# Prompt attention of a hybrid decoder step: stacked score products, turned probabilities as the moving operand, and segments taken from the projection's output

## What is computed

```python
s = einsum('btgrd,bngd->bgrtn', q, kc[:, :, 0]) * HEAD_DIM ** -0.5   # compressed: 31 tokens
p = masked_softmax(s, blk_last[None, :] <= qpos[:, None])
o_cmp = einsum('bgrtn,bngd->btgrd', p, kc[:, :, 1])
# selected and window: the same with 512 keys, and a causal mask
attn = gates[..., 0, None] * o_cmp + gates[..., 1, None] * o_sel + gates[..., 2, None] * o_win
```

## Time and profile before

| | us |
|---|---|
| three timed runs | 3175.24, 3179.0, 3216.62 |
| their median | 3179.0 |
| profiled execution, span (the only time the page gives for it) | 3309.7 |
| TensorE busy | 3073.8 (93%) |
| VectorE busy | 1112.6 (34%) |
| ScalarE busy | 779.8 (24%) |
| GpSimd busy | 144.8 (4%) |

### The profile page before, as it was taken

One profiled execution on the slowest core, in us unless ns is written; L12 is line 12 of the kernel. 1 busy time (PEld: TensorE's weight loads), 2 busy tenths in 40 slices (PEclk: granted clock), 3 DMA queues, 4 the chain that ended last, 5 costly groups with the idle time before them and its releaser, 6 DMA issues.

```text
span 3309.7 us, 51473 instructions
## 1 busy us (share of the span) xinstructions
PE 3073.8 (93%) x21489; PEld 2752.8 (83%) x21489; DVE 1112.6 (34%) x1546; ACT 779.8 (24%) x1182; POOL 144.8 (4%) x147
## 2 busy tenths in 40 slices
PE   4989999977999997875799999999999999999998
PEld 3559999975666665433799999999999999999998
DVE  2322222233222225357533333333333333333333
ACT  1232111111222222201422222222221312222233
POOL 0000000000000000024011000000000000000001
PEclk9999999986555557967899999999999999999999
DMA  4144233330000006622222222222222223222222
GB/s 180 51 149 143 90 93 90 92 88 2 1 0 1 0 0 229 223 71 83 83 96 78 93 92 89 92 91 89 95 89 91 93 89 95 89 89 94 89 89 90
DMA packets 252180, 288.25 MB, mean 87 GB/s; under 512 B 22061, under 2 KB 244403, under 8 KB 248078
## 3 DMA queue, kind: packets, MB, share of 16 engines
q1 hardware_dynamic: 249510, 241.04, 23.1%
q0 software_dynamic: 2592, 46.14, 3.6%
HBM read 274.73 MB, written 20.71 MB: 89 GB/s over the span
## 4 chain that ended last, share of the span: by engine, by line
PE 88%; DVE 6%; DMA 2%; ACT 2%; issue 1%; SPq 0%; POOL 0%; ACTq 0%; POOLq 0%; DVEq 0%
PE PS L610 62%; PE PS L1032 5%; PE PS L1056 4%; PE PS L382 3%; PE PS L1044 2%; PE PS L1033 2%; DMA seg_raw<-in_cache_kv_cmp,idx_c 1%; PE PS L1340 1%; DVE c_tmp L1642 1%; PE PS L931 1%; DVE seg_ord L464 1%; PE PS L1304 1%; DVE st_s L1878 0%; PE PS L1836 0%; PE PS L368 0%
## 5 line engine op out<-in xcount | busy, mean ns | idle before, releaser
L597 DVE TENSOR_TENSOR w_lo<-w_raw,w_hi 128x1024 fp32r<-128x1024 f32 (+1 forms) x388 | 460.2, 1190 | 1387.9 <-ACT w_hi L591 1386.9
L591 ACT ACTIVATE w_hi<-w_raw 128x1024 fp32r<-128x1024 f32 (+1 forms) x388 | 395.4, 1024 | 1501.1 <-PE PS L610 1501.1
L610 PE MATMUL PS<-h_hi,w_hi 128*128 128x260 f32 x3360 | 675.3, 282 | 7.4 <-DVE w_lo L597 5.1
L610 PE MATMUL PS<-h_lo,w_hi 128*128 128x260 f32 x3360 | 675.3, 282 | 0.0
L610 PE MATMUL PS<-h_hi,w_lo 128*128 128x260 f32 x3360 | 674.1, 282 | 0.0
L610 PEld LDWEIGHTS PS<-h_hi,w_hi 128*128 128x128 f32 x3360 | 516.4, 189 | 8.2 <-issue 7.5
L610 PEld LDWEIGHTS PS<-h_lo,w_hi 128*128 128x128 f32 x3360 | 519.1, 189 | 0.0
L610 PEld LDWEIGHTS PS<-h_hi,w_lo 128*128 128x128 f32 x3360 | 518.3, 189 | 0.0
L610 PE MATMUL PS<-u_hi,w_hi 128*128 128x260 f32 x2048 | 411.1, 282 | 8.4 <-DVE u_lo L2223 8.4
L610 PE MATMUL PS<-u_lo,w_hi 128*128 128x260 f32 x2048 | 410.5, 282 | 0.0
L610 PE MATMUL PS<-u_hi,w_lo 128*128 128x260 f32 x2048 | 409.9, 281 | 0.0
(11 more groups left out here) (379 smaller groups left out, 2628.0 us busy)
## 6 DMA issues: line engine op xcount, KB each, us to landing
w_raw<-in_w_up SPq DMA_DIRECT2D x256, 256.0 KB, 2.8
w_raw<-in_w_down SPq DMA_DIRECT2D x256, 256.0 KB, 2.8
w_raw<-in_w_in SPq DMA_DIRECT2D x160, 256.0 KB, 2.9
w_raw<-in_w_out SPq DMA_DIRECT2D x64, 256.0 KB, 3.0
out_kv_win_s<-in_state_kv_win SPq DMA_DIRECT2D x8, 1022.0 KB, 7.4
win_t<-in_state_kv_win SPq DMA_DIRECT2D x16, 448.0 KB
xtok<-in_x_prompt SPq DMA_DIRECT2D x4, 1024.0 KB, 9.2
x_r<-in_x_prompt SPq DMA_DIRECT2D x4, 1024.0 KB, 6.1
```

What stands on the lines that cost most here:

```text
L591: ins = e.activation(hi, raw, ACT.Copy)
L597: ins = e.tensor_tensor(lo, raw, hi.bitcast(F32), ALU.subtract)
L610: mm = e.matmul(PS[:, bank + 2 * m + h, 0:HN], w, x[:, k0 + k, h * HN:h * HN + HN], start=st and c == 0, stop=sp and c == 2)
```

## The change

- **Segments.** `segp`, its trip through memory, the reordering and the 64 transposes go. ACT and DVE copy the segments straight from `pt` into `segp_T`, two copies each. `cmp_w1` is fetched first on SP's queue when the projection ends.
- **Stacked operands.** For each head `q_st` holds 128 rows: the high part of the 64 scaled query rows in one half and the low part in the other. For each branch and group `k_hh` holds the high part of the keys in both halves, `k_ll` the low part in both. ACT makes the high parts (24 activations), DVE the rest (16 scalar_tensor_tensor, 16 subtractions, 8 copies). A score product is then two fp32r products of full height, with no fp32 product. The same for the compressed keys (`kc_hh`, `kc_ll`).
- **Units.** There are 32, one for each head and branch, with all four query tiles in the four banks 0 to 3. After the exponentials GpSimd multiplies the probabilities by gate over row sum in place. The 10 transposes go to banks 4, 5 and 6 by key tile; ACT copies the first, DVE the other two.
- **Values.** 128 columns of values (two key/value heads) are the weights, and the turned probabilities of a key tile stream past: 512, 384, 256 and 128 columns. Both branches and the compressed one add up in bank 7; DVE copies the 64 rows that belong to the head into `mixf`. `att`, its adds on GpSimd, `att_mix_*` and a swap product of the samples go.
- **Order.** `gate_*` comes ahead of the compression's products, `stack_*` ahead of them on ACT and DVE; the 16 small query copies of the samples (`q_dve`) come ahead of `att_cmp_dve`. The gathers of the samples wait for the last score product; the loads of their window rows for the last copy into `mixf`.

Cut to its core:

```diff
-            e.tensor_scalar(pt[:, T_Q:T_Q + 8, :], pt[:, T_Q:T_Q + 8, :], HD ** -0.5, None,
-                            ALU.mult).then_inc(q_scaled, 1)
...
+            segments(e, 0, lambda a, b: e.tensor_copy(a, b), p_seg_d)
...
+        def segments(e, same, copy, done):
+            for a in range(2):
+                x = a if same else 1 - a
+                src = pt[a * HD:a * HD + HD, T_KC:T_KC + 4, 0:SEQ].rearrange("p t (s j x) -> p x t j s", j=8, x=2)
+                dst = segp_T[x * HD:x * HD + HD].rearrange("p (t a) j s -> p a t j s", a=2)
+                copy(dst[:, a], src[:, x]).then_inc(done, 1)
...
+        def stack_act(e):
...
+                        e.activation(q_st[rows_, 8 * x + 4 * a + y, :], pt[rows_, T_Q + 4 * x + y, 0:SEQ], ACT.Copy,
+                                     scale=HD ** -0.5).then_inc(as_hi, 1)
...
+                    e.activation(k_hh[x][y][rows_, :], pt[rows_, K_TILE[x] + y // 2, 0:SEQ],
+                                 ACT.Copy).then_inc(as_hi, 2)
+        def stack_dve(e):
...
+                        e.scalar_tensor_tensor(out=q_st[other, h, :], in0=pt[rows_, T_Q + 4 * x + y, 0:SEQ],
+                                               scalar=HD ** -0.5, in1=q_st[rows_, h, :].bitcast(F32), op0=ALU.mult,
+                                               op1=ALU.subtract).then_inc(as_lo, 1)
...
+                    for to in (rows_, other):
+                        e.tensor_tensor(k_ll[x][y][to, :], src, hh[rows_, :].bitcast(F32), ALU.subtract)
+                    e.tensor_copy(hh[other, :], hh[rows_, :].bitcast(F32)).then_inc(as_lo, 2)
...
+        NU = 2 * NH
+        def score(e, u, qt):
+            h, b = divmod(u, 2)
+            if u:
+                e.wait_ge(as_exp, 4 * (u - 1) + qt + 1)
+            w, g = (qt + 1) * P, h // 4
+            q = q_st[:, h, qt * P:w]
+            e.matmul(PS[:, qt, 0:w], q, k_hh[b][g][:, 0:w], start=True, stop=False)
+            e.matmul(PS[:, qt, 0:w], q, k_ll[b][g][:, 0:w], start=False, stop=False)
+            e.matmul(PS[:, qt, qt * P:w], id_r[:], cm_r[:], start=False, stop=True).then_inc(as_s, 1)
...
             def turn(u):
+                e.wait_ge(as_sc, 4 * (u + 1))
...
+                for n, kts in enumerate(((0,), (1, 3), (2,))):
+                    if u and n == 0:
+                        e.wait_ge(as_ta, u)
+                    elif u:
+                        e.wait_ge(as_td, 2 * (u - 1) + n)
...
             def values(u):
...
+                c = (1 + b) * KVW + KVW // 2 + (h // 8) * P
+                for kt in range(4):
+                    last = e.matmul(PS[:, 7, kt * P:SEQ], kv_tok[:, kt, c:c + P], probT(u, kt),
+                                    start=(b == 0 and kt == 0), stop=False)
+                if b:
...
+                    for qt in range(4):
+                        last = e.matmul(PS[:, 7, qt * P:qt * P + P], vbd[:, h // 8, qt, :], pcT(h),
+                                        start=False, stop=(qt == 3))
...
+            for u in range(NU):
+                factors(u)
+                if u + 1 < NU:
+                    row_max(u + 1)
+                if u and u % 2 == 0:
+                    head_out(u // 2 - 1)
+                turned(u)
...
         def att_pool(e):
+            for u in range(NU):
+                e.wait_ge(as_fac, u + 1)
                 for qt in range(4):
+                    p = prob[:, u % 2, P_OFF[qt]:P_OFF[qt] + (qt + 1) * P]
+                    e.tensor_scalar(p, p, fac[:, u % 2, qt:qt + 1], None, ALU.mult).then_inc(as_sc, 1)
```

More of the change, by code:

```diff
@@ L842, in cmp_p_act @@
                              bias=bias1[:, c:c + 1]).then_inc(p_silu.sem, 1)
+            kcp_high(e)
         def cmp_p_dve(e):
[L845 to L850, removed]
             for c in range(2):
@@ L896, in q_of @@
-        def q_of(head, qt):
-            g, r = head // 4, head % 4
-            a = g % 2
-            return pt[a * HD:a * HD + HD, T_Q + (g // 2) * 4 + r, qt * P:qt * P + P]
-        def k_of(tile0, g, keys):
-            a = g % 2
-            return pt[a * HD:a * HD + HD, tile0 + g // 2, keys]
+        q_st = at("q_st", [P, NH, SEQ], M_RING, F32R)
+        tile_at = lambda t: A2 + t * TILE
+        K_AT = ([(tile_at(2 * g), tile_at(2 * g + 1)) for g in range(NKV)],
+                [(tile_at(14), tile_at(15)), (tile_at(18), tile_at(19)), (tile_at(12), tile_at(13)),
+                 (tile_at(16), A1 + 30720)])
@@ new lines, in build_program @@
+        k_hh, k_ll = ([[at(f"k_{n}{b}{g}", [P, SEQ], K_AT[b][g][x], F32R) for g in range(NKV)] for b in range(2)]
+                      for x, n in enumerate(("hh", "ll")))
+        SB = MF + 11648
+        gates = at("gates", [P, 4, 48], SB)
+        gates_s = at("gates_s", [NB, 48], SB + 768)
+        cm_r = at("cm_r", [P, P], SB + 960, F32R)
+        id_r = at("id_r", [P, P], SB + 1472, F32R)
+        negmax = at("negmax", [P, 2, 4], SB + 1984)
+        den = at("den", [P, 2, 4], SB + 2016)
@@ new lines, in att_cmp_act @@
+                    h = 4 * (g - 1)
+                    for half in range(2):
+                        pair = kv_tok[:, h % 8 // 2 + half, KVW * (1 + h // 8):KVW * (1 + h // 8) + 2 * P]
+                        last = e.activation(pair, PS[:, 6, half * 256:half * 256 + 256], ACT.Copy)
+                    last.then_inc(ac_Tc, 1)
+        NU = 2 * NH
[8 more added lines that the diff above has]
+            e.matmul(PS[:, qt, qt * P:w], id_r[:], cm_r[:], start=False, stop=True).then_inc(as_s, 1)
@@ L1059, in values @@
                 last.then_inc(as_pv, 1)
-            scores(0)
             for u in range(NU):
                 if u + 1 < NU:
-                    scores(u + 1)
+                    for qt in range(4):
+                        score(e, u + 1, qt)
                 if u:
@@ new lines, in head_out, with turned @@
+            def head_out(h):
+                e.wait_ge(as_pv, 2 * (h + 1))
+                a, half = h // 4 % 2, h % 2
+                e.tensor_copy(mixf[half * HD:half * HD + HD, h // 2, 0:SEQ],
+                              PS[a * HD:a * HD + HD, 7, :]).then_inc(as_o, 1)
+            def turned(u):
+                if u >= 2:
+                    e.wait_ge(as_pv, u - 1)
+                e.wait_ge(as_T, 3 * u + 2)
+                both = kv_tok[:, 1, 0:512] if u % 2 == 0 else pt_x[:]
+                e.tensor_copy(both, PS[:, 5, :]).then_inc(as_td, 1)
+                e.wait_ge(as_T, 3 * u + 3)
+                e.tensor_copy(probT(u, 2), PS[:, 6, 0:256]).then_inc(as_td, 1)
@@ L2406, in _ @@
             rows_pe(e)
+            gate_pe(e)
             cmp_p_pe(e)
-            gate_pe(e)
             att_cmp_pe(e)
```

422 lines of the change are left out of this document (188 added, 234 removed).

## The result

| | before | after |
|---|---|---|
| timed runs | 3175.24, 3179.0, 3216.62, 3312.19 | 3081.94, 3085.18, 3085.94, 3092.72 |
| median | 3197.81 | 3085.56 |
| profiled execution, span | 3309.7 | 3090.9 |

The ratio is 0.970, with an interval from 0.964 to 0.976; it leaves out the run of before at 3312, a time that the three runs on record ahead of the prediction did not reach and the profiled span (3309.7) did. The kernel is 3% faster; the forecast of 2930 was 156 us too low. The time lies inside the whole range of 2890 to 3110, but 116 us above the forecast's own range, which ended at 2970. The span fell by 219 us, the median by 112.

A forecast was written before the change was run, and what follows sets the result against it. TensorE's instruction time at the lower clock was taken to bound the heads; 799 + 195 + 3 + 10 + 5 = 1012 against 1265.80, 254 us less, gave 2930 us from the median; own range 2890 to 2970, whole 2890 to 3110.

The forecast's parts named there:

- Taking the 254 off the median gives 2925: Whole kernel: the 254 us gain worked out on the profiled span, subtracted from the timed median of 3179.0.
- rival 1: Heads: the timed runs of before were already partly at the upper clock, so only 123 us gained, 3056; 30%.
- GpSimd's scaling: Heads: four in-place scalings of the probabilities, 1280 elements a unit, priced at 1.8 us, bounds 1.7 and 3.6.
- The ring: Heads: transposes, DVE copies, factor, hand-overs and GpSimd scaling in turn, 4.6 us a unit, 6.4 at GpSimd's upper bound.
- Rivals 3 and 4: Heads: mixed clock or ring leading, 9 us a unit, 3018, 8%; GpSimd's scaling as pace, 17.8 us, 3300, 2%.
- TensorE's own sum: Heads: scores, masks, transposes, values and compressed values total 5.54 us a unit; 6.1 with 10% for turnarounds.
- rival 2: Heads: the new stage stays at 1.2 GHz, 371 us instead of 195, time 3104; 15%.
- The start: Ahead of the heads: compressed scores from 750 against 752.27, the 22 us won almost all given back to DVE.
- The tail: Behind the heads: 32 transposes and a 3.5 us wait go; sample score products take 10 us, then 5 more.
- before the loop stands at 807: Start of the heads: first transposes forecast at 799, set against 807 in the kernel before.
- half-height scores and 64-column values: Heads: what ran at clock 0.50 for 430 us; both gone, so full clock was expected.
- The rule that transposes don't engage the fast clock: Heads: transposes, a fifth of a unit, could keep the stage at the low clock; judged not refuted by the trace.

The follow-up runs named there:

- experiment 1: The kernel before, unchanged, timed and profiled again: 3169.76, 3172.55, 3211.6 and 3293.75 us.
- experiment 4: The rebuilt kernel with DVE making the factors of the next unit right after its maxima, one step earlier: 3046.1 us.
- experiment 7: The rebuilt kernel with the stacked keys made after the compression's DVE and ScalarE steps, queries still before: 3077.0 us.
- Experiments 2: The kernel before with 128 instead of 64 moving columns in the heads' value products, outputs overlapping: 3120.6 us.
- experiment 3: The kernel before with the heads' score products taking all 128 rows, two heads' products added: 3086.8 us.
- experiment 10: The rebuilt kernel with each score product as one fp32 product of 64 rows, low parts left out: 3144.1 us.
- experiment 9: The kernel before with the heads' score products taking all 128 rows, the other head group's keys zero: 3081.6 us, ratio 0.964.
- experiment 6: The rebuilt kernel with DVE scaling the 384- and 512-column query tiles, GpSimd only those of 128 and 256: 3041.4 us.

## Why the prediction was wrong

**The step that failed** is "Taking the 254 off the median gives 2925". It takes a difference worked out against a span with all 16 heads at the lower clock off a median whose runs had only some of them there. The gap of 131 us between span and median was in the text, and what it was stood there as rival 1, with 30% and 3056. I took the other reading, that recording slows all instructions; experiment 1 shows it does not (the span is 1.8 us from the time), and that the gap is the number of heads at the lower level times 12.26 us. Against that median only 254 - 131 = 123 us were to be had, and the measured 3085.6 is 30 us above the 3056 that this gives. Profile against profile, where the level of the clock is known, the shortfall is 35 us, and the points that follow account for it.

**GpSimd's scaling was mis-sized.** I took 1.8 us a unit with bounds of 1.7 and 3.6; it measured 4.27, outside both. The rows that I drew on were a one-input copy (1.3 ns an element) and a two-input product (2.8); an instruction with a scalar per partition takes 2.5 ns an element and 0.28 us to start, and there are four. The ring around it was right in its parts: 2.8 us beside GpSimd forecast, 2.64 measured. The sum of ring and price was therefore 6.91 instead of TensorE's 6.1, 26 us over 32 units. Rivals 3 and 4 named the place, at 9 and 17.8 us a unit; the size lay between them and the forecast, which gave GpSimd's bound 10 us at most.

**Right:** TensorE's own sum: 5.54 us a unit forecast, 5.41 measured once GpSimd was out of the way (experiment 4), with nothing for turnarounds, where I had added 10%. Its terms, in the chain of experiment 4: scores with masks 1.80 forecast, 1.66 measured; transposes 1.12 and 1.09; values 2.17 and 2.21; compressed values 0.90 and 0.89 a head. The clock of the new stage: 1.00 from 820 to 1000 us (0.91 in 1000 to 1020, at its end), 1.00 in the middle of it in two more profiles of the new kernel, and the mean clocks of its other runs are as high (0.951 to 0.957); rival 2 did not happen. The start: scores at 750 forecast, 751.95 measured, and most of what was won ahead given back to the stacking, as experiment 7 shows. The tail: 15 us from the heads to the key transposes forecast, 14.3 measured. Profile against profile the forecast was -254, the measurement -219; 23 of the missing 35 are in the heads (198 forecast, 220.7 measured), 5.5 in the samples' attention, which I had left unchanged, 3 in the start, and 3 in a projection that ended later.

**A reading that was off:** "before the loop stands at 807" is the first score product of the heads, and I set it against first transposes at 799. The first transposes of before are at 810.3. The gain ahead of the heads in my own terms was 11 us, not 8, and measured it was 8.4.

**Half right:** what keeps the clock low. I named half-height scores and 64-column values together. Experiments 2 and 3 show that, in the kernel before, removing either is enough; experiment 10 shows that the rebuilt kernel with half-height fp32 scores does not stay at the upper level throughout, in spite of its wide value products. The rule that transposes don't engage the fast clock, cited from the Trainium skill (TensorE: Matmul & The Clock Gate, Part 4), did not decide here: the stage holds 20 transposes a head before and after, and in both kernels it was at 1.00 with them (before from 1030 on in experiment 1, after from 820 to 1000).

**Not seen at all:** that products of 64 rows also cost issue time at a given clock, 2.2 us a head (experiment 3). This part of the gain, as that of the clock, needed none of the stacking (experiment 9).

## What to carry to other kernels

Before you subtract a gain worked out from one profile from a median, ask at which level of the clock the profile was and at which the timed runs; here 16 heads could cost 235 us (worked out, 16 x 14.67) or 431 with the same instructions, and the gap between span and median was the sign. Where TensorE is busy all the time at the lower level, first try the smallest edit that makes its products full height or wider, zeros included, and only then rebuild; in this kernel either was enough. When a change hands a step to another engine, look where the first wait on it stands in each queue: one line of order was worth 45 us of the stage here, against 112 in the median for the whole rebuilding.

## What the runs showed of the hardware

- The granted clock went from 0.50 (1000 to 1020) over 0.93 (1020 to 1030) to 1.00 in the middle of a periodic stage, with nothing different in the instructions and TensorE busy 100% at both levels. Within the heads it did not fall back in the profile that shows it (0.97 in 1100 to 1140); behind them, in 1140 to 1150, it was 0.50 again. By their times (3136 to 3319 us for one kernel) other runs had more or fewer heads at the lower level; no trace shows where.
- A score group of 512 fp32 columns with its mask: 1.31 us with 64 rows, 0.92 with 128, at clock 1.00.
- Value products with 128 moving columns instead of 64: 14.81 against 14.67 us a head, for 40 such products.
- GpSimd's tensor_scalar with a scalar per partition: 0.60, 0.92, 1.24, 1.56 us for 128 to 512 fp32 elements. DVE's: 0.42 and 0.60 us for 384 and 512 (experiment 6).
- A copy of 1024 elements in each of 64 partitions, read with a stride of 16, took ScalarE 1.95 us and DVE 1.08 (`segp_T`, two each).
